# Transposes in the RWKV block inverse: four 128x128 transposes in place of sixteen 64x64 products

## What is computed

```python
def step(state, inp):
    r_t, w_t, k_t, v_t, a_t, b_t = inp
    sa = jnp.einsum('bhvk,bhk->bhv', state, a_t)
    state = state * w_t[:, :, None, :] + sa[..., None] * b_t[:, :, None, :] + v_t[..., None] * k_t[:, :, None, :]
    y = jnp.einsum('bhvk,bhk->bhv', state, r_t)
    return state, y
```

## Time and profile before

| | |
|---|---|
| median of three runs | 1534.05 us |
| the profiled execution, its own time | 1534.71 us |
| its span | 1532.9 us |
| TensorE busy | 1429.8 us (93%) |
| VectorE busy | 549.7 us (36%) |
| ScalarE busy | 300.0 us (20%) |
| GpSimd busy | 114.9 us (7%) |
| TensorE's share of the chain of waits that ended last | 87% |
| mean granted TensorE clock | 0.971 |
| the inverse, first to last level | 1054.8 to 1246.9 us |

### The profile page before, as it was taken

How to read it: one execution, slowest core, us unless ns; L and a number is a source line. 1 busy time by engine, 2 the same in 40 slices (tenths; PEclk the granted TensorE clock), 3 DMA queues, 4 the chain that set the end, 5 groups by cost and what they waited for, 6 DMA issues and landing times.

```text
span 1532.9 us, 23984 instructions
## 1 busy us (share of the span) xinstructions
PE 1429.8 (93%) x10700; PEld 1039.4 (68%) x10700; DVE 549.7 (36%) x1020; ACT 300.0 (20%) x631; POOL 114.9 (7%) x180
## 2 busy tenths in 40 slices
PE   7999679899999997799999988998888899999999
PEld 6875447668886444458888447866777765888843
DVE  5546441122222024713333018365544354233300
ACT  2210210201110021612121002602333331121200
POOL 5526000000000000000000000011100000000000
PEclk9999869999999998899999998999999999999999
DMA  8434104144443344033444341410000142344342
GB/s 316 165 111 165 55 0 165 56 138 158 165 162 130 147 165 164 0 117 137 157 165 162 132 182 73 172 48 3 4 31 4 31 167 77 143 165 150 132 157 83
DMA packets 16614, 182.11 MB, mean 119 GB/s; under 512 B 1648, under 2 KB 3824, under 8 KB 5888
## 3 DMA queue, kind: packets, MB, share of 16 engines
q1 hardware_dynamic: 14320, 175.12, 31.2%
q10 hardware_dynamic: 2192, 5.46, 1.0%
HBM read 179.52 MB, written 1.05 MB: 118 GB/s over the span
## 4 chain that ended last, share of the span: by engine, by line
PE 87%; DVE 7%; issue 3%; ACT 3%; POOL 0%; DMA 0%; DVEq 0%; POOLq 0%
PE banks L1172 37%; PE banks L1405 14%; PE banks L1203 12%; PE banks L1182 4%; PE banks L1632 3%; PE banks L1356 2%; PE banks L1621 2%; ACT weight_ring L1064 1%; PE banks L1158 1%; PE banks L1527 1%; PE banks L1493 1%; DVE weight_ring L2425 1%; PE banks L1746 1%; PE banks L1697 1%; PE banks L1330 1%
## 5 line engine op out<-in xcount | busy, mean ns | idle before, releaser
L1172 PE MATMUL banks<-hT,weight_ring 128*128 128x256 f32 x2240 | 488.4, 380 | 1.0 <-DVE hT L1892 1.0
L1172 PEld LDWEIGHTS banks<-hT,weight_ring 128*128 128x128 f32 x2240 | 425.8, 190 | 61.9 <-issue 1.2
L1405 PE MATMUL banks<-weight_ring,arena 128*128 128x512 f32 x528 | 227.4, 592 | 0.0
L2168 DVE SCALAR_TENSOR_TENSOR arena<-banks,prm,arena 128x255 f32<-128x255 f32 x220 | 96.1, 478 | 305.4 <-ACT arena L908 197.2
L1405 PEld LDWEIGHTS banks<-weight_ring,arena 128*128 128x128 f32 x528 | 100.3, 190 | 123.9 <-issue 123.7
L1203 PE MATMUL banks<-weight_ring,arena 128*128 128x512 f32 x288 | 125.3, 593 | 1.8 <-ACT arena L889 1.0
L1901 DVE TENSOR_TENSOR x<-x,banks 128x512 f32<-128x512 f32 x28 | 19.2, 686 | 275.1 <-PE banks L1405 194.1
L1203 PEld LDWEIGHTS banks<-weight_ring,arena 128*128 128x128 f32 x288 | 54.2, 190 | 67.4 <-issue 66.4
L908 ACT ACTIVATE arena<-banks,prm 128x256 f32<-128x256 f32 x66 | 33.6, 559 | 242.0 <-PE banks L1172 207.8
L1172 PE MATMUL banks<-arena,weight_ring 128*128 128x256 f32 x320 | 72.9, 391 | 0.2 <-DVE arena L2031 0.2
L1172 PEld LDWEIGHTS banks<-arena,weight_ring 128*128 128x128 f32 x320 | 62.5, 196 | 10.8 <-issue 2.0
(11 more groups left out here) (382 smaller groups left out, 1410.0 us busy)
## 6 DMA issues: line engine op xcount, KB each, us to landing
weight_ring<-in_wall SPq DMA_DIRECT2D x81, 2048.0 KB, 8.0
weight_ring<-in_wall SPq DMA_DIRECT2D x2, 1024.0 KB, 7.2
x<-in_x_tok ACTq DMA_DIRECT2D x2, 512.0 KB, 4.3
arena<-in_mem_tok SPq DMA_DIRECT2D x1, 1024.0 KB, 18.1
arena<-in_wall SPq DMA_DIRECT2D x1, 1024.0 KB, 6.2
arena<-in_wide SPq DMA_DIRECT2D x2, 512.0 KB, 4.6
out_y<-x ACTq DMA_DIRECT2D x4, 256.0 KB, 2.0
arena<-in_masks ACTq DMA_DIRECT2D x1, 896.0 KB, 10.3
```

What stands on the lines that cost most here:

```text
L1172: ins = mm(b_(n)[:, j * T:(j + 1) * T], lhsT=wc[:, kb * 512 + c0:][:, :P], rhs=xT[:, kb, :], start=kb == 0, stop=kb == blocks - 1)
L1405: ins = mm(b_(tile_group(name, tt, c)), lhsT=actT[:, fb, tt * P:(tt + 1) * P], rhs=wc[:, (fb % 4) * D + c * 512:][:, :512], start=fb == 0, ...
L2168: ins = stt(out, src, col(f"fcw{i}", tap * nb_ + fb), out, ALU.mult, ALU.add)
```

## The change

T moves to the column order "k b c", so that the two sides of tile k lie side by side as 128 columns, one whole 128x128 block. The groups `tt` and `tf` become four 128x128 transposes each, of T's four blocks, into the first bank of their pair. Transposing a 128x128 block swaps side and partition half at once, so the four results hold the same tiles as before in another order, and ScalarE's copy (`evict_turned`) reads them with a pattern that puts them into `Tt` and `Tf` as before. The `yl` and `tl` groups, their order and all waits are as they were; `Tc` is now a view with runs of 64 columns, which VectorE, GpSimd and `four_tiles` use.

```diff
+        def turned_(n):
+            return bank[BANK_OF[n]].rearrange("p (k b c) -> p b k c", k=4, b=2)
...
-        Tc, Tt, Yb = [[quads(half_of(ap, h)) for h in HALVES]
-                      for ap in (lent[:, 2, 0, 0:1024], lent[:, 2, 0, 1024:2048], lent[:, 2, 1, 0:1024])]
+        T_rows = [half_of(lent[:, 2, 0, 0:1024], h) for h in HALVES]
+        Tc = [ap.rearrange("p (k b c) -> p b k c", k=4, b=2) for ap in T_rows]
+        Tt, Yb = [[quads(half_of(ap, h)) for h in HALVES] for ap in (lent[:, 2, 0, 1024:2048], lent[:, 2, 1, 0:1024])]
...
+            def evict_turned(dst, n):
+                act.wait_ge(psum_full, n + 1)
+                A(dst, turned_(n), ACT.Copy).then_inc(bank_sem(n), 1)
...
                     evict_pair(Yb[h], G[f"yl{j}{lv}{h}"])
-                    evict_pair(Tt[h], G[f"tt{j}{lv}{h}"])
+                    evict_turned(Tt[h], G[f"tt{j}{lv}{h}"])
...
-                    evict_pair(Tf[h], G[f"tf{j}{h}"])
+                    evict_turned(Tf[h], G[f"tf{j}{h}"])
...
+            def turn(n, blocks_):
+                for k in range(4):
+                    ins = nc.tensor.transpose(b_(n)[:, k * P:(k + 1) * P], blocks_[:, k * P:(k + 1) * P], ident)
+                ins.then_inc(psum_full, 1)
...
                     n = G[f"tt{j}{lv}{h}"]
                     free(n)
-                    four_tiles(n, blocks(Tc[h]), unit)
+                    turn(n, T_rows[h])
...
                     pe.wait_ge(*when_read(G[f"tl{j}{LEVELS - 1}{h}"]))
-                    four_tiles(n, blocks(Tc[h]), unit)
+                    turn(n, T_rows[h])
```

## The result

| | before | after |
|---|---|---|
| median of the runs made together | 1533.60 us (4 runs) | 1519.74 us (4 runs, 1518.78 to 1523.58) |
| ratio, 95% interval | | 0.9913 [0.9897, 0.9928] |
| profiled execution, its span | 1534.71, 1532.9 us | 1519.95, 1518.1 us |
| instructions, mean granted clock | 23984, 0.971 | 21296, 0.972 |

The kernel became 0.9% faster: 13.9 us between the medians, 14.8 between the two profiled executions. The sign of the forecast held, and the time lies in its range, but the gain is about twice the 7.1 us that the sum gave.

The account below looks back on a forecast made before the run. TensorE was taken to run short of instruction blocks in the block inverse, with ScalarE's copies pacing unstopped levels. Terms -10.2 + 4.6 - 1.5 = -7.1 us gave a median of 1527.0 us, range 1519 to 1540.

Parts of the forecast that it names:

- the first term: Block inverse: 2688 fewer TensorE records let instruction blocks come just soon enough, so the 12.6 us of stops mostly go: -10.2 us.
- term (5): Granted clock in the inverse: with the idle stop gone, the stretch at 1.2 GHz goes too: -1.5 us.
- one stop of 1.5 us: Inverse levels: one stop was kept because blocks need 5.7 us against some 6.3 us of work, a thin margin.
- The 0.9 us of waits that would return: In 3 of 20 levels a stop hid a wait for ScalarE, which comes back: 3 x 0.31 us.
- 8 to 10 were forecast: Sign to look for in the stage: waits for ScalarE's copies rise to about 8 to 10 us.
- The transposes' time: Inverse levels: each set of four transposes takes 0.24 us longer through the change of array shape: +4.6 us in all.
- Final transposes, copies, layout: Final transposes stay covered by VectorE's copies, and copies in runs of 64 take no longer: 0 us.
- the forecast's 0.45: Chance given to the main forecast, whose own range is 1522 to 1532 us; three quarters counted as faster by over 0.3%.
- B: Rival: more gain than forecast; all stops and the slow clock go, transposes cost nothing: 1520 us, chance 0.17.
- A: Rival: the stops stay, from another cause or blocks still late; only slower transposes are left: +3 us, 1537, chance 0.2.
- C: Rival: the clock falls to 1.2 GHz in levels with transposes; slower, 1556 us with 10 of 20 levels, chance 0.1.
- D: Rival: VectorE's copies in the first pass, next in line, take the gain: 1531 us, no change, chance 0.08.

Follow-up runs that it names:

- experiment 5: The kernel before with each set of in-level transposes as four 256-column products in the old array shape, three quarters of the transposes left out: 1520.26 us, ratio 0.9911.
- experiment 8: The changed kernel with both Y groups of a level ahead of both sets of transposes: 1521.11 us, ratio 0.9923.
- (1): The kernel before with T in the new column order, but the old 64x64 products and the old copy pattern: 1533.95 us, ratio 0.9996.
- experiments 5 and 7: The first is experiment 5; the second is the kernel before with an idle 352-column product heading each level of passes 1 and 2 alone: 1536.20 us.
- experiments 2 and 6: First: new transposes for half 0 only within levels, final ones both new, 1528.91 us. Second: kernel before with an idle 352-column product heading each level, 1544.72 us.
- experiment 9: The changed kernel with both sets of transposes of a level ahead of both Y groups: 1519.78 us, ratio 0.9907.

## Why the prediction was right or wrong

**The step that failed is the first term**, the -10.2 us for the record count, with the -1.5 of the clock beside it: the cause and the direction were right, the size was not. The runs give -16.0 us in their place.
- It took the "issue" row of the waits, 12.6 us, for all that the stops cost. That row counts idle time from the modelled end of the last product, 0.22 us after its start, while products in a run start every 0.01 to 0.04 us. From one instruction to the next, the same 14 stops last 15.7 us. To this come stops of other lines (0.7 us on line 1746, two of 0.3 on lines 1621 and 1632), and what fell where something else would have been waited for goes off again. The levels alone got 14.3 us back, and 1.7 came between them: with term (5), -11.7 were forecast, and -16.0 came.
- It left one stop of 1.5 us, as the margin was thin; none came. The margin was about right: 1.5 blocks in a level at 3.8 us, 5.7 us, against some 6.3 for the level and its key products.
- The 0.9 us of waits that would return did return: in experiment 5, with the stops gone and the old shape, ScalarE's row is 6.2 us against 5.3. In the changed kernel it is 3.1, where 8 to 10 were forecast, because TensorE spends on the transposes the time in which it would have waited.
- **The transposes' time** was right in kind: 0.24 us a set, a level of 3.97 where 3.99 was forecast. It costs 3.3 us where 4.6 were forecast: nine levels pay 0.27 to 0.47 us, 2.8 together, and the other eleven 0.05 on average, where 12 by 0.32 and 8 by 0.1 were assumed. The rule of the Trainium skill that changing the tiling mode drains TensorE (TensorEngine Tiling (Array Packing), Key Properties) agrees with two runs: without the change of shape (experiment 5) the fastest level is 3.67 us again, and with half as many changes (experiment 8) it is 3.71 against 3.96.
- **Final transposes, copies, layout**: next to nothing, as forecast. ScalarE's copies are 599 and 598 ns by the two lines against 600, VectorE's masked copy 734 against 731. For the layout there is a run of its own (1). The final transposes are covered at the end of pass 1, and at the end of the last pass they are 0.4 us shorter.
- **The clock**: the stage's granted clock went from 0.99 to 1.00. That term is inside the -16.0; it was not tried by itself.
- **The chances**: three quarters of the forecast's 0.45 are 0.34 and not 0.36, so faster by over 0.3% should have had 0.53.

Of the rivals, **B** came nearest with 1520, though by other terms: it gave nothing for the transposes and the stops 14.1 us; they were +3.3 and -16.0. **A**, the stops stay, is refuted by the change and by experiments 5 and 7. The rule of the Trainium skill behind it (Runtime: NRT & Kernel Launch, Instruction fetch mechanics), that fetching is hidden behind dispatch, doesn't hold in this kernel: 256 instructions of 64x64 products run in 1.9 us, and no two transfers of a block started less than 3.2 us apart. Its unit of 256 instructions agrees to the instruction. **C**, a falling clock, did not happen in the changed kernel: with 192 transposes in the stage it stayed at 1.00, so the rule that transposes don't count as activity (TensorE: Matmul & The Clock Gate, Part 4) had no effect that the stage shows. But TensorE at 1.2 GHz, the loss that C feared, came behind the long stops of experiments 2 and 6, after a lack of instructions and not after transposes. **D**, VectorE's copies in the first pass take the gain, did not happen: the five levels of that pass fell from 25.0 to 22.3 us. VectorE took 0.4 us, in its norm chain behind the stage.

## What to carry to other kernels

Where "issue" waits stand among dense small matmuls, count TensorE's instructions between them: if it is a multiple of 256, as in this kernel, fewer instructions per microsecond is the cure, even if each of them is slower, and work may be added there at little cost. Look again at an "issue" wait that falls elsewhere: in experiment 9 twenty of 23 belonged to ScalarE. The row of such waits may fall short of what they cost; measure from one instruction to the next across each stop. And look at the granted clock of a trace before you judge a small change by it: 1.9 us won by a better order were lost again where TensorE ran at half the clock for a few microseconds.

## What the runs showed of the hardware that was not expected

- TensorE's program comes in blocks of 256 instructions of 16 KB, one held ahead. In 14 traces the transfers of two blocks never started less than 3.2 us apart, and each stop of over 0.3 us at a block end of the stage ended 2.2 to 2.8 us after its block's transfer had started.
- With 2 MB weight tiles on their way at about 400 GB/s, the next block's transfer started 2.3 to 4.1 us after a block end (13 traces, in twelve of them 3.2 or more), in place of 0.8 to 2.6 us at the stops of the kernel before. Where the block in hand was used up first, that made stops of 2.33 and 3.45 us.
- The stop of 2.33 us was followed by the lower level of the clock: 0.67 granted over 15.4 us that were worked through without a pause. Behind the stop of 3.45 us it was 0.50 over the next 6.1 us.
- The shape of the array costs at each change, not by the number of instructions: four transposes of 128x128 between 64x64 products take 0.24 us more than the 16 products (64 records) that they replace, and both sets together, with one change there and back, save 0.25 us of a level.
